# Earlier first gathers, a split last gather, full-partition compression and a reordered query norm in a two-layer transformer kernel

## The chip, the cores and the metric

The kernel runs on one core of one Trainium2 chip. The metric is the device time of one launch in microseconds (us). Three runs of the kernel before gave 3327.53, 3336.08 and 3337.21 us (median 3336.08).

## The reference

The input is a sequence of 256 tokens of width 2048, in float32. Two layers and a last norm are computed.

```python
# layer 1: four attention groups of 8 heads of 64 each, then an MLP
u = rmsnorm(h, norm_attn); p = split(u @ w_in)
o_mla = mla_mixer(...)      # c_q is normed (q_norm) before w_uq
o_fox = fox_mixer(...)      # forgetting attention, bias from a cumulative sum
o_nsa = nsa_mixer(...)      # compressed + selected + windowed attention
o_swa = swa_mixer(...)      # windowed, with sinks
h = h + rmsnorm(concat(o)) @ w_out
h = h + square(relu(rmsnorm(h) @ w_up)) @ w_down

def nsa_compress(kv, pos_emb, w1, w2):     # for keys and for values, 2 kv heads
    blk = kv[:, :, idx] + pos_emb          # 15 windows of 32 tokens, stride 16
    return gelu(blk.reshape(b, g, 15, 32 * 64) @ w1) @ w2

# layer 2: retention + RG-LRU, cross-attention to 256 memory rows, then experts
def peer_ffn(xn, w_q, sub_keys, u_tab, v_tab):
    q = xn @ w_q                            # 8 heads x 2 halves of 128
    vals, ids = top_k(q . sub_keys, 16)     # per token, head and half, of 128 keys
    top_sc, pos = top_k(vals0 + vals1, 16)  # of the 256 pairs
    eid = id0 * 128 + id1                   # 128 experts for each token
    act = gelu(x . u_tab[eid])              # 2048-long dot products
    return sum(softmax(top_sc) * act * v_tab[eid])
```

The last step is `rms_norm(h, final_norm)`.

## The kernel before

All engines run programs written out by hand and are tied by semaphores. Activations stand transposed, width on the 128 partitions and the 256 tokens on the free axis. Large products go in "chunks": a weight load of 1 MB lands in a ring of three slots (issued by SP), ACT rounds each half of it (128 x 1024) into `wh`, DVE takes the remainder into `wl` (L1690), and TensorE does three matmuls for each of 8 k-tiles of a half (L555 to L557; L617 to L619 with tokens as rows). Three halves of `wh`/`wl` rotate. `weave` interleaves the projections with the mixers on every engine by fixed ratios of `yield` steps, so what an engine does next is fixed by the code.

**The start of the mixers.** TensorE turns a column of factors (L517) and then wants the squares of the query latent `cq` for its norm (L498, `norm_sums`). In ACT's `mixers()` the copy of the factors, the copy of the bias row (`brow`), and the issue of its DMA come ahead of `squares("cq", cq)`.

**The compression.** `kc` and `vc` hold both kv heads, head g on partitions 64g to 64g+63. DVE builds `blk` (128 x 32 x 15, four additions at L1921), then TensorE does, for keys and again for values, 32 positions x 2 heads matmuls with 64 rows, 64 columns of weights and 15 moving columns (L782); a gelu on ACT and a second small product (L793, L798) follow. The relative-position biases (3 loads of 1 MB from DRAM into `bias`, issued by POOL at L2356) wait until the outputs of the first two mixers (`cqm`, which lives in `bias`) are moved away by DVE (L1908).

**The experts.** `first_queries` computes the queries of head 0 for token tile 0 (L955), their scores against the sub-keys (L1008), and turns the normed rows (L1000). DVE's `topk(0)` then gives 16 expert numbers a token (`eid`, L2248). There are 256 "rows" n (2 token tiles x 128 experts); for each, POOL issues an indirect DMA (L2368) that brings for 128 tokens one row of the table `uv` (2 MB: 2048 of u, 2048 of v). Row n lands in a buffer `BUF[n]`; five buffers rotate up to row `FEW` = 80, seven after it. A gather waits until the row that last used its buffer is added. DVE does the dot product (L2261, `dot`), ACT three small steps (`weigh`: gelu, times gate, a diagonal of weights), TensorE four matmuls of 512 columns (L1025, `sum_row`) that add into one of two PSUM tiles `sums`. Between rows TensorE does quarter chunks of the remaining queries (L981, `steps_before(n)` of them before row n, 16 before row 0), their weights coming through SP (`in_w_pq`, 1 MB each). The top-16 of later heads runs on DVE in four pieces before rows n with n % 16 in `TOP_AT` = (0, 2, 4, 6). `finish(t)` norms the sums of a tile: a square over 2048 columns with its sum on ACT, a mean on DVE, a root on ACT (after a table load), reciprocal and two products of 1024 columns on DVE (L2273), and two stores through SP (L2416).

## Time and profile before

| | us |
|---|---|
| median of three runs | 3336.08 |
| profiled execution | 3331.21 |
| its span | 3329.4 |
| PE / DVE / ACT / POOL busy | 3042.9 / 1924.9 / 1279.9 / 372.0 |

The profiled execution is 1.8 us longer than its span. By the page's row of DMA tenths the DMA engines are about half busy up to slice 24 of 40 (some 2000 us) and full from there to the last slice; TensorE is at nine tenths up to the same place and at seven tenths after it. A busy engine isn't the bound by itself: what counts in each stage is which wait ends last.

### The profile page before, as it was taken

To read this page: it belongs to the slowest core of one execution; us is meant where nothing else is said; L and a number is where in the kernel's file an instruction comes from. 1 tells how busy PE (TensorE), PEld (TensorE's weight loads), DVE (VectorE), ACT (ScalarE), POOL (GpSimd) and SP (SyncE) were. 2 spreads that over 40 slices of the span, in tenths; PEclk is the share of its full clock that TensorE was granted. 3 is DMA by queue.
4 is the path that set the end of the run, shared out by engine and by line. 5 is a ranking of instruction groups with operands and counts; after the bars stand their busy time and mean duration, and the time that the engine had idled before them with its cause. 6 is when DMAs were issued, how large, how long until landed. Compare 5 with 4: busy or idle time off the path is not lost.

```text
span 3329.4 us, 43391 instructions
## 1 busy us (share of the span) xinstructions
PE 3042.9 (91%) x18036; PEld 2379.4 (71%) x18036; DVE 1924.9 (58%) x2872; ACT 1279.9 (38%) x2355; POOL 372.0 (11%) x364
## 2 busy tenths in 40 slices
PE   8999999999999999999999999999987777777776
PEld 8888978999999999989999997444442233333332
DVE  6565665555555555676765454555555555555654
ACT  4554554444434345565544352222222222222222
POOL 1001000000000001100000011222232222222221
PEclk9999999999999999999999999999999989999999
DMA  7454446555555555544445448999999999999997
GB/s 216 174 195 158 161 151 215 179 188 179 188 179 186 181 182 198 195 165 153 152 177 203 140 152 333 430 431 430 431 430 431 430 429 431 431 431 431 431 431 337
DMA packets 94785, 912.65 MB, mean 274 GB/s; under 512 B 10416, under 2 KB 14904, under 8 KB 19580
## 3 DMA queue, kind: packets, MB, share of 16 engines
q0 software_dynamic: 38128, 541.61, 38.1%
q1 hardware_dynamic: 48816, 344.95, 29.9%
q10 hardware_dynamic: 7644, 23.30, 2.2%
q8 instruction: 142, 2.33, 0.3%
q14 instruction: 55, 0.45, 0.0%
HBM read 900.38 MB, written 9.45 MB: 273 GB/s over the span
## 4 chain that ended last, share of the span: by engine, by line
PE 66%; DMA 23%; DVE 6%; ACT 4%; issue 1%; ACTq 0%; POOL 0%; DVEq 0%; POOLq 0%
PE sums L555 15%; PE sums L557 14%; PE sums L556 14%; DMA area<-in_uv,cst 13%; PE sums L1025 9%; DMA hT<-in_uv,cst 5%; DMA ringx<-in_uv,cst 3%; PE sums L981 2%; DVE area L2261 1%; PE sums L617 1%; DVE wl L1690 1%; PE sums L619 1%; PE sums L618 1%; ACT cst L1070 1%; ACT area L1070 1%
## 5 line engine op out<-in xcount | busy, mean ns | idle before, releaser
L1690 DVE TENSOR_TENSOR wl<-ring,wh 128x1024 fp32r<-128x1024 f32 x612 | 749.9, 1230 | 597.2 <-ACT wh L1070 596.3
L1070 ACT ACTIVATE wh<-ring 128x1024 fp32r<-128x1024 f32 x612 | 643.5, 1054 | 460.2 <-PE sums L557 404.5
L1070 ACT ACTIVATE cst<-cst 128x1 f32<-128x1 f32 (+2 forms) x786 | 234.2, 299 | 903.6 <-DVE cst L2261 845.1
L1025 PE MATMUL sums<-area,cst 128*128 128x512 f32 x984 | 457.4, 611 | 100.1 <-ACT cst L1070 99.8
L1025 PEld LDWEIGHTS sums<-area,cst 128*128 128x128 f32 x984 | 182.7, 193 | 356.6 <-issue 189.6
L2261 DVE CUSTOM_DVE_ANT_0 area<-area 128x2048 f32<-128x2048 f32 x123 | 281.8, 2291 | 254.5 <-DMA area<-in_uv,cst 254.5
L555 PE MATMUL sums<-normed,wh 128*128 128x256 f32 x1440 | 407.0, 283 | 0.2 <-DVE wl L1690 0.2
L557 PE MATMUL sums<-normed,wl 128*128 128x256 f32 x1440 | 406.7, 282 | 0.0
L1025 PE MATMUL sums<-ringx,cst 128*128 128x512 f32 x656 | 303.8, 609 | 60.0 <-ACT cst L1070 60.0
L555 PE MATMUL sums<-hidden,wh 128*128 128x256 f32 x1024 | 289.8, 283 | 0.0
L556 PE MATMUL sums<-hidden,wh 128*128 128x256 f32 x1024 | 289.8, 283 | 0.0
L557 PE MATMUL sums<-hidden,wl 128*128 128x256 f32 x1024 | 289.8, 283 | 0.0
L556 PE MATMUL sums<-normed,wh 128*128 128x256 f32 x1024 | 289.8, 283 | 0.0
L2261 DVE CUSTOM_DVE_ANT_0 ringx<-ringx,area 128x2048 f32<-128x2048 f32 x82 | 187.9, 2291 | 170.7 <-DMA ringx<-in_uv,cst 170.7
L1025 PEld LDWEIGHTS sums<-ringx,cst 128*128 128x128 f32 x656 | 122.0, 192 | 229.4 <-issue 127.5
L555 PEld LDWEIGHTS sums<-normed,wh 128*128 128x128 f32 x1440 | 275.6, 191 | 0.5 <-issue 0.5
L557 PEld LDWEIGHTS sums<-normed,wl 128*128 128x128 f32 x1440 | 275.6, 191 | 0.0
L555 PE MATMUL sums<-inputs,wh 128*128 128x256 f32 x896 | 261.4, 292 | 2.2 <-DVE wl L1690 2.2
L557 PE MATMUL sums<-inputs,wl 128*128 128x256 f32 x896 | 253.3, 283 | 0.0
L2339 POOL TENSOR_TENSOR ssq<-ssq,sqb 128x256 f32<-128x256 f32 x75 | 56.4, 752 | 1661.2 <-ACT sqb L1070 1659.1
L556 PE MATMUL sums<-inputs,wh 128*128 128x256 f32 x848 | 239.8, 283 | 0.0
L2368 POOL DMA_INDIRECT area<-in_uv,cst x123 | 146.5, 1191 | 471.4 <-PE sums L1025 452.9
(335 smaller groups left out, 5753.6 us busy)
## 6 DMA issues: line engine op xcount, KB each, us to landing
ring<-in_w_in_a SPq DMA_DIRECT2D x66, 1024.0 KB, 4.9
ring<-in_w_up SPq DMA_DIRECT2D x64, 1024.0 KB, 4.9
ring<-in_w_down SPq DMA_DIRECT2D x64, 1024.0 KB, 4.9
ring<-in_w_out SPq DMA_DIRECT2D x32, 1024.0 KB, 5.0
ring<-in_w_in_b SPq DMA_DIRECT2D x16, 1024.0 KB, 4.9
ring<-in_w_xk SPq DMA_DIRECT2D x16, 1024.0 KB, 5.2
ring<-in_w_xv SPq DMA_DIRECT2D x16, 1024.0 KB, 5.1
ring<-in_w_xq SPq DMA_DIRECT2D x16, 1024.0 KB, 5.0
```

Source lines behind the costliest of these rows:

```text
L555: te.matmul(bank[:, 0:T], wh[:, j % 3, x], hi[:, k, :], start=k == 0, stop=False)
L556: te.matmul(bank[:, 0:T], wh[:, j % 3, x], lo[:, k, :], start=False, stop=False)
L557: mm = te.matmul(bank[:, 0:T], wl[:, j % 3, x], hi[:, k, :], start=False, stop=k == 15)
L617: te.matmul(b[t][:, :], hi[:, k, y], wh[:, j % 3, x], start=k == 0, stop=False)
L618: te.matmul(b[t][:, :], hi[:, k, y], wl[:, j % 3, x], start=False, stop=False)
L981: mm = te.matmul(bank[:, y], slots3[s][:, k * P:(k + 1) * P], xn[:, k, y], start=k == 0, stop=k == 15)
L1025: mm = te.matmul(sums[t][:, 512 * i:512 * i + 512], diag[:, n % 2, :], v[:, 512 * i:512 * i + 512], start=False, stop=n % 128 == 127)
L1070: return sc.activation(out, in_, f, **kw)
L1690: ve.tensor_tensor(wl[:, j % 3, :], ring[:, load % 3, j % 2 * 1024:j % 2 * 1024 + 1024], wh[:, j % 3, :], ALU.subtract).then_inc(lo_in, 1)
L2261: ve.tensor_tensor_reduce(u, u, xrow[:, t, :], 1.0, 0.0, ALU.mult, ALU.add, dots[:, t, s:s + 1]).then_inc(dotted, 1)
L2339: gp.tensor_tensor(acc[:, :], acc[:, :], sqb[:, j % 4, :], ALU.add).then_inc(acc_in, 1)
L2368: gp.indirect_dma_start(rowbuf[BUF[n]], None, A["uv"], bass.IndirectOffsetOnAxis(ap=eid[:, t, s:s + 1], axis=0)).then_inc(rows_in[BUF[n]], 16)
```

## The change

1. Experts, first rows: the scores of head 0, tile 0 are computed and evicted in two halves, the first in the middle of the second query chunk. `first_two()` gives the expert numbers of rows 0 and 1 right after the first eight of each half are known (the best pair, and the better of the two next candidates), so POOL gathers these two rows ahead of the rest of the top-16. DVE has nine more small instructions there.
2. Experts, order: 12 quarter chunks before row 0 instead of 16, then one for each row up to 5, then one for every two rows; five buffers up to row 110 instead of 80; the pieces of the top-16 stand before rows 8 to 11 of each 16 for the first seven, then at 0, 2, 4, 6 as before. ACT evicts scores after a row's weights instead of before them.
3. Experts, end: row 255 is gathered in two halves: u into its buffer, v (behind row 249) into the upper half of another. TensorE counts its four matmuls one by one; ACT squares 512 columns at a time with the root's table loaded ahead; DVE multiplies by the gain before the factor is known; the last factor is applied in two halves, 1024 columns by ACT and 1024 by DVE, stored by two queues.
4. Compression: weights and positions are laid out so that even and odd positions share the 128 partitions. TensorE first swaps the partition halves of `kc` and `vc` by four matmuls of 256 columns; DVE makes `blk` with eight additions of 64 x 8 x 15 for each of keys and values, before the copies of the mixer outputs; TensorE then does 16 matmuls of 128 rows, 64 weight columns and 30 moving columns for each instead of 64.
5. Biases: `cqm` moves out of `bias`; the three bias loads become six of half the size, the first three behind the forgetting rows, the last three once the second mixer has used its scores.
6. ACT's `squares("cq", cq)` comes before the copies and the DMA issue.
7. `cst` loses a table that was not used, so one early load falls from 1623 KB to 855 KB.

```diff
-        FEW = 80
-        BUF = ([0, 1, 2, 3, 4] * (FEW // 5) + [5, 0, 1, 2, 3, 4, 6] * 26)[:256]
+        FEW = 110
+        BUF = ([0, 1, 2, 3, 4] * (FEW // 5) + [5, 0, 1, 2, 3, 4, 6] * 21)[:256]
...
-        TOP_AT = (0, 2, 4, 6)
+        LATE = 249
+        def top_at(g):
+            return (8, 9, 10, 11) if g < 7 else (0, 2, 4, 6)
         def steps_before(n):
-            return min(64, 16 + 5 * n // 8)
+            return 12 + n if n < 5 else min(65, 17 + (n - 5) // 2)
...
+                off(on, EVICTED["nsa"] - 1)
+                on.wait_ge(out_off, 8)
+                for j, src in enumerate((kc, vc)):
+                    for g in range(2):
+                        mm = te.matmul(banks[6 + j][64 - 64 * g:128 - 64 * g, T:2 * T], ident[:, 64 * g:64 * g + 64],
+                                       src, start=True, stop=True)
+                    mm.then_inc(cmp_mm, 1)
...
-                    on.wait_ge(cmpw_in[j], 16 * len(cmp_w[j]))
-                    on.wait_ge(out_off, 8)
-                    on.wait_ge(blk_in, 2 * j + 2)
-                    for l in range(32):
-                        w, at = (cmp_w[1][1], l - 20) if j and l >= 20 else (cmp_w[j][0], l)
-                        for g in range(2):
-                            r = slice(64 * g, 64 * g + 64)
-                            mm = te.matmul(banks[6 + j][r, 0:15], w[r, at * 64:at * 64 + 64], blk[r, l, :],
-                                           start=l == 0, stop=l == 31)
+                    on.wait_ge(cmpw_in[j], 16)
+                    on.wait_ge(blk_in, 8 * j + 8)
+                    for i in range(16):
+                        mm = te.matmul(banks[6 + j][0:64, 0:30], cmp_w[j][:, i * 64:i * 64 + 64], blk[j][:, i, :],
+                                       start=i == 0, stop=i == 15)
                     mm.then_inc(cmp_mm, 1)
                     yield
-                    w2 = w2p[:, 64 * j:64 * j + 64]
+                    w2 = w2p[0:64, 64 * j:64 * j + 64]
...
+                        elif k == 8:
+                            on.wait_ge(keys_in, 16)
+                            on.wait_ge(qp_in, 1)
+                            on.wait_ge(rd_mean, RD_MEANS["ffn"])
+                            sub_scores(0, (0,), (0,))
...
-                on.wait_ge(keys_in, 16)
                 on.wait_ge(qp_in, 2)
-                on.wait_ge(rd_mean, RD_MEANS["ffn"])
-                sub_scores(0, (0,))
+                sub_scores(0, (0,), (1,))
                 off(on, len(EVICTIONS) - 1)
...
+                b, nth = (BUF[LATE], NTH[LATE] + 1) if n == 255 else (BUF[n], NTH[n])
+                v = rowbuf[b][:, DM:2 * DM]
                 on.wait_ge(weighed, n + 1)
+                on.wait_ge(rows_in[b], 16 * nth)
                 for i in range(4):
                     mm = te.matmul(sums[t][:, 512 * i:512 * i + 512], diag[:, n % 2, :], v[:, 512 * i:512 * i + 512],
                                    start=False, stop=n % 128 == 127)
-                mm.then_inc(added, 1)
+                    if n == 255 or i == 3:
+                        mm.then_inc(added, 1)
             biases()
...
+                on.wait_ge(off_v, EVICTED["cq"])
+                squares("cq", cq)
                 column(1)
                 on.wait_ge(brow_mm, 1)
                 act(brow[0:16, :], banks[3][0:16, :], ACT.Copy).then_inc(brow_in, 1)
...
+            def finish_last():
+                on.wait_ge(fin_v, 3)
+                act(pst[:, 3:4], ident[:, 0:1], ACT.Sqrt).then_inc(a_seq, seq.one())
+                for i in range(4):
+                    y = slice(512 * i, 512 * i + 512)
+                    on.wait_ge(added, 256 + i)
+                    act(xrow[:, 1, y], sums[1][:, y], ACT.Square, accum_out=sq4[:, i:i + 1]).then_inc(fin_a, 1)
+                on.wait_ge(fin_v, 7)
+                on.wait_ge(a_seq, seq.n)
+                act(pst[:, 3:4], pst[:, 2:3], ACT.Sqrt).then_inc(fin_a, 1)
+                on.wait_ge(fin_v, 9)
+                act(final[1][:, 0:1024], final[1][:, 0:1024], ACT.Copy, scale=pst[:, 3:4]).then_inc(fin_a, 1)
+                on.wait_ge(fin_a, 8)
+                sc.dma_start(A["out"][P:2 * P, 0:1024], final[1][:, 0:1024]).then_inc(out_in, 16)
...
+            def blocks(j, src):
+                on.wait_ge(small_in, 32)
+                off(on, EVICTED["nsa"] - 1)
+                on.wait_ge(cmp_mm, j + 1)
+                own, swapped = (x.rearrange("p (c l) -> p l c", l=16) for x in (src, banks[6 + j][:, T:2 * T]))
+                for s in range(2):
+                    r = slice(64 * s, 64 * s + 64)
+                    for g in range(2):
+                        x = own if g == s else swapped
+                        for a in range(2):
+                            at = slice(8 * a, 8 * a + 8)
+                            ve.tensor_tensor(blk[j][r, at, 15 * g:15 * g + 15], x[r, s::2, a:a + 15],
+                                             w2p[r, 128 + 16 * j + 8 * a:136 + 16 * j + 8 * a].unsqueeze(2)
+                                             .to_broadcast([64, 8, 15]), ALU.add).then_inc(blk_in, 1)
...
+            def first_two():
+                x = eq[:, 0, :]
+                own(ve.tensor_copy(idf[:, :, 0:2], ids[:, :, 0:2]))
+                on.wait_ge(v_seq, seq.n)
+                ve.scalar_tensor_tensor(eid[:, 0, 0:1], idf[:, 0, 0:1], 128.0, idf[:, 1, 0:1], ALU.mult,
+                                        ALU.add).then_inc(eid_in, 1)
+                for a in range(2):
+                    b = 1 - a
+                    own(ve.tensor_tensor(x[:, a:a + 1], vals[:, 0, a:a + 1], vals[:, 1, b:b + 1], ALU.add))
+                    own(ve.scalar_tensor_tensor(x[:, 2 + a:3 + a], idf[:, 0, a:a + 1], 128.0, idf[:, 1, b:b + 1],
+                                                ALU.mult, ALU.add))
+                on.wait_ge(v_seq, seq.n)
+                own(ve.tensor_tensor(x[:, 4:5], x[:, 0:1], x[:, 1:2], ALU.is_ge))
+                own(ve.tensor_tensor(x[:, 5:6], x[:, 2:3], x[:, 3:4], ALU.subtract))
+                on.wait_ge(v_seq, seq.n)
+                ve.scalar_tensor_tensor(eid[:, 0, 1:2], x[:, 5:6], x[:, 4:5], x[:, 3:4], ALU.mult,
+                                        ALU.add).then_inc(eid_in, 1)
...
-                on.wait_ge(scr_in, h + 2 if g else 1)
+                if g:
+                    on.wait_ge(scr_in, h + 3)
                 for c in range(2):
+                    if g == 0:
+                        on.wait_ge(scr_in, c + 1)
                     s = scr[:, h, 256 * t + P * c:256 * t + P * c + P]
                     own(ve.max(vals[:, c, 0:8], s))
                     on.wait_ge(v_seq, seq.n)
                     own(ve.max_index(ids[:, c, 0:8], vals[:, c, 0:8], s))
                     on.wait_ge(v_seq, seq.n)
+                    if g == 0 and c == 1:
...
+                if g == 15:
+                    x = eq[:, 0, 0:1]
+                    own(ve.scalar_tensor_tensor(x, sel[:, 0, 15:16], 128.0, sel[:, 1, 15:16], ALU.mult, ALU.add))
+                    on.wait_ge(v_seq, seq.n)
+                    for a in range(2):
+                        own(ve.tensor_scalar(eid2[:, a:a + 1], x, 2.0, float(a), ALU.mult, ALU.add))
+                    on.wait_ge(v_seq, seq.n)
+                e0 = 0 if g else 2
+                ve.scalar_tensor_tensor(eid[:, t, 16 * h + e0:16 * h + 16], sel[:, 0, e0:16], 128.0,
+                                        sel[:, 1, e0:16], ALU.mult, ALU.add).then_inc(eid_in, 1)
...
+            def finish_last():
+                on.wait_ge(grow_in, 16)
+                def times(i):
+                    y = slice(512 * i, 512 * i + 512)
+                    on.wait_ge(fin_a, 3 + i)
+                    ve.tensor_tensor(final[1][:, y], sums[1][:, y], grow[:, y], ALU.mult).then_inc(fin_v, 1)
+                for i in range(3):
+                    times(i)
+                on.wait_ge(fin_a, 6)
+                own(ve.tensor_reduce(pst[:, 2:3], sq4, AX.X, ALU.add))
+                on.wait_ge(v_seq, seq.n)
+                ve.tensor_scalar(pst[:, 2:3], pst[:, 2:3], 1.0 / DM, EPS, ALU.mult, ALU.add).then_inc(fin_v, 1)
+                times(3)
+                on.wait_ge(fin_a, 7)
+                ve.reciprocal(pst[:, 3:4], pst[:, 3:4]).then_inc(fin_v, 1)
+                on.wait_ge(fin_v, 9)
+                ve.tensor_scalar(final[1][:, 1024:2048], final[1][:, 1024:2048], pst[:, 3:4], None,
+                                 ALU.mult).then_inc(fin_v, 1)
...
+            def biases(h):
+                for x, d in ((0, 0), (1, 1), (2, 0)):
+                    view = bass.AP(bias_d.tensor, h * 128 * 513 + 255 - 128 * d, [[512, 128], [128 * 513, 8], [1, 128]])
+                    gp.dma_start(bias[:, h:h + 8, x * 128:x * 128 + 128], view).then_inc(bias_in, 16)
...
+            biases(0)
+            on.wait_ge(bias_in, 48)
+            on.wait_ge(biased, 16)
+            biases(8)
...
-                on.wait_ge(eid_in, n // 16 + 1)
-                gp.indirect_dma_start(rowbuf[BUF[n]], None, A["uv"],
-                                      bass.IndirectOffsetOnAxis(ap=eid[:, t, s:s + 1], axis=0)
-                                      ).then_inc(rows_in[BUF[n]], 16)
+                on.wait_ge(eid_in, n + 1 if n < 2 else n // 16 + 3)
+                if n < 255:
+                    gp.indirect_dma_start(rowbuf[BUF[n]], None, A["uv"], which(eid[:, t, s:s + 1])).then_inc(rows_in[BUF[n]], 16)
+                else:
+                    gp.indirect_dma_start(rowbuf[BUF[n]][:, 0:DM], None, halves, which(eid2[:, 0:1])
+                                          ).then_inc(rows_in[BUF[n]], 16)
+                    on.wait_ge(added, LATE + 1)
+                    gp.indirect_dma_start(rowbuf[BUF[LATE]][:, DM:2 * DM], None, halves, which(eid2[:, 1:2])
```

The order of DVE's instructions around the compression, before; `m1l` is the remainder of the memory rows, `wl` that of a weight half, `xn` takes the mixer outputs, `blk` the windows:

```order
L1744 SCALAR_TENSOR_TENSOR m1l<-area,x1l 128x256 x8
L1690 TENSOR_TENSOR wl<-ring,wh 128x1024
L1908 COPY xn<-area 128x256 x4
L1690 TENSOR_TENSOR wl<-ring,wh 128x1024
L1908 COPY xn<-area 128x256 x4
L1690 TENSOR_TENSOR wl<-ring,wh 128x1024
L1912 TENSOR_SCALAR nsink<-sinks 128x8
L1690 TENSOR_TENSOR wl<-ring,wh 128x1024
L1921 TENSOR_TENSOR blk<-area,w2p 128x240 x2
L1690 TENSOR_TENSOR wl<-ring,wh 128x1024
L1921 TENSOR_TENSOR blk<-area,w2p 128x240 x2
```

and after (`area` holds the windows there):

```order
L1779 SCALAR_TENSOR_TENSOR m1l<-area,x1l 128x256 x8
L1725 TENSOR_TENSOR wl<-ring,wh 128x1024
L1895 TENSOR_TENSOR area<-area,w2p 64x8x15 x2
L1895 TENSOR_TENSOR area<-sums,w2p 64x8x15 x4
L1895 TENSOR_TENSOR area<-area,w2p 64x8x15 x2
L1962 COPY xn<-cst 128x256 x4
L1725 TENSOR_TENSOR wl<-ring,wh 128x1024
L1895 TENSOR_TENSOR area<-area,w2p 64x8x15 x2
L1895 TENSOR_TENSOR area<-sums,w2p 64x8x15 x4
L1895 TENSOR_TENSOR area<-area,w2p 64x8x15 x2
L1962 COPY xn<-cqm 128x256 x4
L1725 TENSOR_TENSOR wl<-ring,wh 128x1024
L1965 TENSOR_SCALAR nsink<-sinks 128x8
L1725 TENSOR_TENSOR wl<-ring,wh 128x1024 x4
```

Sixteen shorter additions now stand ahead of the copies and of two `wl`, and none stands behind the last one shown.

TensorE's order where the experts begin, before: L955 is a query chunk of tile 0, L1008 scores, L1000 the turned rows, L981 query chunks, L1015 the residual that starts the sums, L1025 the weighted rows of v:

```order
L961 MATMUL sums<-cst,ssq 128x1 x2
L955 MATMUL sums<-xn,ring 128x128 x16
L1008 MATMUL sums<-area 128x128 x2
L1000 MATMUL sums<-cst,xn 128x128 x32
L981 MATMUL sums<-xn,ring 128x128 x32
L1008 MATMUL sums<-area 128x128 x2
L981 MATMUL sums<-xn,ring 128x256 x32
L1008 MATMUL sums<-area 128x128 x4
L1015 MATMUL sums<-cst,hT 128x128 x16
L1025 MATMUL sums<-area,cst 128x512 x8
L981 MATMUL sums<-xn,ring 128x256 x4
```

and after (the same steps are L968, L1023, L1015, L999, L1030 and L1042):

```order
L974 MATMUL sums<-cst,ssq 128x1 x2
L968 MATMUL sums<-xn,ring 128x128 x8
L1023 MATMUL sums<-area 128x128
L968 MATMUL sums<-xn,ring 128x128 x8
L1023 MATMUL sums<-area 128x128
L1015 MATMUL sums<-cst,xn 128x128 x32
L999 MATMUL sums<-xn,ring 128x128 x32
L1023 MATMUL sums<-area 128x128 x2
L999 MATMUL sums<-xn,ring 128x256 x16
L1030 MATMUL sums<-cst,hT 128x128 x16
L1042 MATMUL sums<-area,cst 128x512 x4
L999 MATMUL sums<-xn,ring 128x256 x4
```

The first scores moved into the middle of the second chunk, and one wide chunk and four score matmuls now stand behind the first rows instead of ahead of them.

ACT's last instructions, before:

```order
L1070 ACTIVATE cst<-cst 128x1 x2
L1070 ACTIVATE cst<-cst 128x128
L1070 ACTIVATE area,cst<-sums 128x2048
L1070 ACT_TABLE_LOAD
L1070 ACTIVATE cst<-cst 128x1
```

and after:

```order
L1088 ACTIVATE cst<-cst 128x1 x2
L1088 ACTIVATE cst<-cst 128x128
L1088 ACT_TABLE_LOAD
L1088 ACTIVATE cst<-cst 128x1
L1088 ACTIVATE area,cst<-sums 128x512 x4
L1088 ACTIVATE cst<-cst 128x1
L1088 ACTIVATE xn<-xn,cst 128x1024
L1581 DMA out<-xn 128x1024
```

The table load and a first root stand ahead of the squares, and a product and a store have come to ACT.

## Rows read from the trace of the kernel before

**Rows 1.** Windows: us, length, busy of each engine, PE clock, DMA share, GB/s

```profile
600.00:1000.00 400.00, 400.00 (x3334) 399.95 (x3333) 216.50 (x263) 177.85 (x221) 4.43 (x6) 1.00 0.54 182
2200.00:2400.00 200.00, 183.09 (x522) 97.65 (x523) 113.15 (x181) 46.56 (x138) 45.69 (x39) 0.98 1.01 431
2800.00:3270.00 470.00, 362.94 (x771) 142.39 (x770) 268.34 (x392) 101.08 (x308) 105.03 (x96) 0.98 1.01 431
```

**Rows 2.** Timeline of PE: start, us, instruction; idle before it, releaser

```profile
57.24 0.50 PE L517 MATMUL sums<-cst,rd 128*128 128x1 f32 x4
59.78 2.53 PE L498 MATMUL sums<-sqb,cst 128*128 128x256 f32 x6 [2.04 <-ACT sqb L1070]
```

**Rows 3.** Timeline of ACT there

```profile
57.98 0.59 ACT L1070 ACTIVATE area<-sums 16x512 f32<-16x512 f32 x1
58.60 0.67 ACTq L1247 DMA_DIRECT2D bias_rows<-area  x1
59.31 1.03 ACT L1070 ACTIVATE sqb<-area 128x256 f32<-128x256 f32 x3 [0.74 <-ACT area L1070]
```

**Rows 4.** Windows of 10 us where the PE clock falls

```profile
60.00:70.00 10.00, 9.87 (x58) 8.89 (x58) 6.66 (x8) 4.27 (x9) 0.00 (x0) 0.83 0.88 104
300.00:310.00 10.00, 8.00 (x136) 7.79 (x134) 2.12 (x3) 1.42 (x2) 2.10 (x2) 0.63 0.99 316
310.00:320.00 10.00, 9.37 (x162) 8.93 (x162) 2.17 (x3) 1.52 (x3) 0.00 (x0) 0.84 0.50 190
320.00:330.00 10.00, 10.00 (x78) 9.25 (x77) 3.53 (x5) 3.71 (x7) 0.00 (x0) 0.85 0.36 120
```

**Rows 5.** Timeline of PE from the norms to the late heads

```profile
236.34 1.99 PE L498 MATMUL sums<-sqb,cst 128*128 128x256 f32 x8 [0.54 <-ACT sqb L1070]
...
302.26 6.79 PE L782 MATMUL sums<-blk,area 64*64 64x15 f32 x128 [2.00 <-DVE blk L1921]
...
316.21 4.21 PE L782 MATMUL sums<-blk,area 64*64 64x15 f32 x128 [0.63 <-DVE blk L1921]
...
326.44 0.93 PE L669 MATMUL sums<-area 64*128 64x128 f32 x8
```

**Rows 6.** Timeline of DVE there

```profile
293.82 1.75 DVE L1690 TENSOR_TENSOR wl<-ring,wh 128x1024 fp32r<-128x1024 f32 x1
...
301.11 1.01 DVE L1921 TENSOR_TENSOR blk<-area,w2p 128x240 f32<-128x240 f32 x2
```

**Rows 7.** Window around the first gathers

```profile
2018.00:2030.00 12.00, 11.63 (x86) 10.95 (x85) 6.56 (x24) 4.03 (x9) 3.87 (x4) 1.00 0.62 221
```

**Rows 8.** Timelines of PE, DVE and POOL from the first scores to row 5

```profile
2013.41 0.68 PE L1008 MATMUL sums<-area 128*128 128x128 f32 x4 [0.41 <-issue]
...
2014.70 0.29 DVE L2206 MAX8 cst<-area 128x8 f32<-128x128 f32 x1 [3.70 <-ACT area L1070]
...
2024.47 0.17 DVE L2248 SCALAR_TENSOR_TENSOR cst<-cst 128x16 int32<-128x16 f32 x1
...
2044.07 2.27 DVE L2261 CUSTOM_DVE_ANT_0 area<-area 128x2048 f32<-128x2048 f32 x1
...
2024.92 1.04 POOL L2368 DMA_INDIRECT area<-in_uv,cst  x1 [17.34 <-DVE cst L2248]
...
2051.43 1.85 POOL L2368 DMA_INDIRECT area<-in_uv,cst  x1 [20.48 <-PE sums L1025]
```

**Rows 9.** Timelines of DVE, PE and ACT at the end

```profile
3312.93 2.29 DVE L2261 CUSTOM_DVE_ANT_0 ring<-ring,area 128x2048 f32<-128x2048 f32 x1 [2.56 <-DMA ring<-in_uv,cst]
...
3323.79 2.48 DVE L2273 SCALAR_TENSOR_TENSOR xn<-sums,cst,area 128x1024 f32<-128x1024 f32 x2
...
3316.34 3.70 PE L1025 MATMUL sums<-ring,cst 128*128 128x512 f32 x8 [1.16 <-ACT cst L1070]
...
3320.07 1.88 ACT L1070 ACTIVATE area<-sums 128x2048 f32<-128x2048 f32 x1 [3.79 <-PE sums L1025]
...
3322.06 1.28 ACT L1070 ACT_TABLE_LOAD   x1
```

179 lines of the change are left out of this document (82 added, 97 removed).

## Prediction

> **What bounds the kernel now.** I read the windows by stage first, then the waits of the engine that leads in each, then the chain of waits, to see whether such a wait stands on it. Up to about 2005 us TensorE leads: in a stretch of 400 us it is busy for 400.00, with 3334 matmuls, so 0.12 us for each matmul of 256 columns, while the DMA share is 0.54 [rows 1]. There a time counts if TensorE works less, idles less, or keeps its clock. The expert stage is led by the DMA engines: the share is 1.01 at 430 to 431 GB/s, with five buffers (window 2200 to 2400) and with seven (2800 to 3270) [rows 1]. A row of 2.097 MB takes 4.87 us at that rate. In that stage only three things count: when the stream fills, whether it breaks, and what follows its last byte. The change touches both kinds of stage.
>
> **A, query norm first.** TensorE sat idle for 2.04 us before L498, released by ACT's squares [rows 2]. ACT spent that time on the bias row (0.59) and the issue of its DMA (0.67), then squared at 59.31 [rows 3]. Squares first, TensorE can go on right behind L517, some 1.9 us earlier. After the idle the PE clock fell: the window 60 to 70 shows 0.83 [rows 4], that is 1.7 us lost to half clock (1.2 instead of 2.4 GHz). Full gain 3.6. But ACT must round the next weight half and square `ckv` a little later, and TensorE wants both sooner than before; I estimate about 1 us of new wait. I take 2.5, between 0.5 (the wait comes back for the next norm, the clock falls all the same) and 3.6. The bias row's DMA starts some 3 us later; its readers come tens of us after it.
>
> **B, compression.** The stretch from the end of the projections at 300.26 (302.26 less the 2.00 idle) to the late heads at 326.44 lasts 26.2 us [rows 5]. TensorE's order puts 72 projection matmuls in it: 8.6 us at 0.12. The compression takes 6.79 + 4.21 = 11.0, the idles before it 2.00 + 0.63 = 2.6 [rows 5], the small second products 0.7 (estimate). Together 22.9; the other 3.3 are projections at half clock: the windows from 300 to 330 show 0.63, 0.84 and 0.85 [rows 4], and the same 128 passes took 6.79 in the first and 4.21 in the second [rows 5].
> After: 32 passes for each of the two instead of 128. At 33 ns a pass (4.21/128) that is 1.05 us; if twice the rows and columns doubled it, 2.1. I take 1.3 each, 2.6 for both. The swap adds four matmuls of 256 columns, 2.0 us by the like of L498 (1.99) [rows 5], but it stands where TensorE waits for DVE's `m1l` pieces, which it catches up with; I leave 0.35.
> DVE is the new risk. It works without a break there, finishing a `wl` at 295.57 (293.82 + 1.75) [rows 6]. A pair of old additions (240 elements each) took 1.01 us [rows 6]. Eight new ones of 120 elements: at least half of 0.5 each, 2.0 us; at most the same 0.5 each, 4.0. I take 2.5 for keys and 2.5 for values. The first eight stand behind that `wl` and ahead of four copies (0.9) and the next `wl` (1.2), which then ends at 300.1; TensorE wants it at about 298.9, so it idles 1.3 us. The next `wl` ends at 304.7, when TensorE, through with the first compression, wants it at 304.8. Behind DVE's additions are queued only these `wl` halves, and TensorE alone waits for them; ACT isn't held up.
> New stretch: 8.6 + 2.6 + 0.7 + 0.35 + 1.3 = 13.6, a gain of 12.6. With 4.0 us for each eight it is some 5 less, and if the clock falls again for as long as in A, 2 less: 5.5 at the low end. At the high end, with no new idle, 14. I take 12.
>
> **C, first rows.** Now scores start at 2013.41, `topk(0)` at 2014.70, the ids are there at 2024.64 and POOL issues row 0 at 2024.92 [rows 8]. After: the first scores come after 8 of 16 k-tiles, so ACT has them at about 2011.7, DVE is through its first set when the second arrives at 2014.5; two steps (0.7) and the first id (0.4) give 2015.6, and POOL issues row 0 at 2016.0, row 1 at 2017.2. The rest of `topk(0)` ends at 2024.2 for nine more small instructions and the earlier start. What this is worth isn't the 9 us of row 0 but the bytes moved before the stream is full: between 2018 and 2030 the engines moved 221 of 431 GB/s [rows 7], leaving 12 x (1 - 221/431) = 5.8 us free. Two rows (9.7 us) and a query load (2.4) fill that window whole, and rows 2 to 4 follow from 2024.5. Gain 5.5, with 3 if the first gathers start slowly, 7 if they start before 2018.
> Does the stream break later? Rows 0 to 4 and three query loads are 31.6 us of transfers, to about 2049. Row 5 needs row 0 added. Before, `dot(0)` was held until 2044.07 by a piece of the next top-16 and row 5 was issued at 2051.43 [rows 8]. Now no piece stands there, 12 steps instead of 16 stand ahead on TensorE, and row 0 is added at about 2040. So the cover grows. From there a row costs TensorE 3.4 us plus half a step of 1.7, 4.3 under 4.87. The four pieces of a top-16 (10.3 us) and four dots (9.1) fill rows 8 to 11 on DVE, 19.4 of 19.5 us, while four rows of transfers (19.5 us) are in flight behind: a row is added about 7.3 us after it lands, so some 12 us of delay are covered. Cost of item 2: nothing. The new wait of `sum_row` on the buffer holds up only TensorE's own next matmuls and is met when the weight is.
>
> **D, the end.** The last row landed at 3312.93; dot, weight and a wait put its matmuls at 3316.34, 1.16 us after TensorE was free; they end at 3320.04 [rows 9]. With u landing half a row (2.4 us) before v, its weight is ready before TensorE has added row 254. So not 2.4 but only 1.2 are gained. Then 2048 columns of square (1.88 and 0.2 for the sum), a mean, a table load (1.28), a root, a reciprocal and 2.48 of products end at 3326.27 [rows 9]: 6.2 us. After: a square of 512 columns (0.6, estimate from 1.88), the sum 0.2, two small DVE steps 0.3, the last product with the gain 0.65 beside the root, reciprocal 0.15, 1024 columns on ACT 1.05, hops 0.3: 3.3 us. That is 2.9 less, of which I give back 0.9, as both halves of the output now start together instead of 1.2 us apart. D is 1.2 + 2.0 = 3.2, between 1 and 5.
> On the load of the table the row shows 1.28 us and the root at once behind it [rows 9]. The Trainium skill, "ScalarE: Activation LUTs", section "What ACT_TABLE_LOAD costs", adds a drain of about 1.38 us to each switch; by it the early load would save 2.7 and D would be 4.6. The trace shows no such drain, and I stay with 1.28.
> On the split gather the windows show the stream at its full rate with up to five gathers queued [rows 1]. The Trainium skill, "DMA: Bandwidth & Descriptors", section "Anatomy of one DMA — SWDGE (gpsimd) path", gives each transfer some 2.0 us of fixed time beside its bytes. If that were paid in line, the second half would land 2.0 later and D would be 1.2; against it speak the last dots, 4.85 us apart (2.29 and 2.56 idle) with 4.87 us of bytes in each [rows 9].
>
> **E, the rest.** Bias loads in six parts: the same 3 MB, the first 1.5 MB at about 95 to 105 us beside weight loads. The stage's DMA share is about half [rows 1], and a weight slot is refilled more than two halves ahead of its use, so nothing; up to 3 us if a weight load is late. The shorter load of `cst` helps no one who waits.
>
> **Sum.** 2.5 + 12 + 5.5 + 3.2 = 23.2. Against the profiled execution: 3331.2 - 23.2 = 3308.0. That execution stands 4.9 us under the median of the three, and the highest of them 6 over it; I predict **3309**, one us up for that. A difference of 0.3% (10 us) is about what a measurement of this kernel can tell from none; the median less that is 3326.
>
> **Rivals.**
> *TensorE's stages give little* (chance 0.17). DVE's additions take 4 us for each eight, TensorE idles on `wl`, and the idle brings the half clock back, as a wait of 2 us did twice here [rows 2, 4, 5]. Then A is 0.5 and B 5.5: 3331.2 - 0.5 - 5.5 - 5.5 - 3.2 = 3316.5. For it speaks DVE without a gap at 293.8; against it that the new idle is 1.3, and wide matmuls follow it.
> *The experts give nothing* (0.12). Early gathers push the query weights back, TensorE waits for them, buffers come free late, and the end follows from TensorE: C and D are 0, 3331.2 - 14.5 = 3316.7. For it: TensorE is busy 183 of 200 us in the window to 2400 [rows 1]. Against: the cover of 12 us.
> *Both* (0.04): 3331.2 - 6 = 3325.
> *Slower* (0.03). The top-16 pieces before rows 8 to 11 leave DVE 0.1 us of slack. If DVE falls behind by more than the 12 us of cover there, the first row of the next head is gathered late and the DMA engines idle, in each of seven heads. From 3.3 us a head on the whole gain is eaten; at 6 us: 3308 + 42 = 3350.
> *The forecast*: 0.64.
>
> **Numbers.** The forecast's own range is 3300 to 3317; the rivals at 3316 to 3325 stretch the upper side. Runs of one kernel lie 10 us apart, so I give 3297 to 3322. Faster by over 0.3% is nearly all of the forecast and of its first two rivals, less what the spread of the runs takes: 0.88. Within 0.3%: 0.09. Slower: 0.03.
>
> **What would show it.** A: no idle over 1 us before the first norm's matmuls, clock at 1.0 between 60 and 70. B: passes of the compression 1 to 2 us for each, late heads at about 311 to 314. C: the first gather issued some 9 us before the full `topk`, DMA share 1.0 from 2 us behind it, and the time from first gather's data to last landing unchanged per byte. D: 9 us or less from the landing of v to the last byte out. Wrong: any window of the expert stage with a share under 0.98; TensorE waiting for `wl` over 2 us near 300; a low clock near 305.

## The result and the profile after

| | before | after |
|---|---|---|
| median | 3331.81 us (4 runs, 3326.97 to 3337.21) | 3307.97 us (4 runs, 3307.00 to 3311.36) |
| profiled execution, its span | 3331.21, 3329.4 | 3307.08, 3304.7 |

The ratio is 0.9929, 95% interval 0.9917 to 0.9940: faster by 0.7%. The forecast was 3309.

The two traces are compared at landmarks that both have: the column of factors in front of the first norm (L517 / L523), the first chunk behind the norms (L725 / L731), the late heads (the first matmuls of the heads that follow the compression, L669 / L675), the first expert queries (L955 / L968), the landing of row 254 (the start of its dot, which waits for the DMA), the end of the span. The landmarks of before that stand in no group, in timelines of PE and DVE:

```profile
67.86 1.46 PE L725 MATMUL sums<-area 128*96 128x256 f32 x6
...
2005.24 3.73 PE L955 MATMUL sums<-xn,ring 128*128 128x128 f32 x32
...
3308.07 2.29 DVE L2261 CUSTOM_DVE_ANT_0 hT<-hT,area 128x2048 f32<-128x2048 f32 x1 [2.58 <-DMA hT<-in_uv,cst]
```

and in the timeline of PE after, from the first norm to the first queries:

```profile
56.54 0.50 PE L523 MATMUL sums<-cst,rd 128*128 128x1 f32 x4
56.91 1.54 PE L504 MATMUL sums<-sqb,cst 128*128 128x256 f32 x6
...
62.30 0.67 PE L504 MATMUL sums<-sqb,cst 128*128 128x256 f32 x2 [0.97 <-ACT sqb L1088]
...
64.23 1.46 PE L731 MATMUL sums<-area 128*96 128x256 f32 x6
...
287.53 1.08 PE L781 MATMUL sums<-area,cst 128*64 128x256 f32 x8
...
295.64 0.39 PE L561 MATMUL sums<-x1l,wh 128*128 128x256 f32 x1 [0.85 <-DVE wl L1725]
...
297.26 2.05 PE L791 MATMUL sums<-area 128*64 128x30 f32 x32
...
300.86 0.29 PE L802 MATMUL sums<-hk,w2p 64*64 64x15 f32 x4
...
304.13 2.05 PE L791 MATMUL sums<-area 128*64 128x30 f32 x32
...
311.12 0.93 PE L675 MATMUL sums<-area 64*128 64x128 f32 x8
...
1990.53 3.73 PE L968 MATMUL sums<-xn,ring 128*128 128x128 f32 x32
```

The idle of 2.04 us before the norm [rows 2] is gone and one of 0.97 has come at the next norm. Of the compression's 128 passes 32 are left, 2.05 us in all, and only 0.85 us of idle stands ahead. The PE clock no longer falls in any window that stood at 0.63 to 0.85 [rows 4] (us, length, busy of each engine, PE clock, DMA share, GB/s):

```profile
60.00:70.00 10.00, 9.03 (x65) 8.13 (x63) 7.01 (x10) 6.87 (x12) 0.00 (x0) 1.00 0.76 89
300.00:310.00 10.00, 10.00 (x100) 9.43 (x100) 3.39 (x3) 3.04 (x6) 0.00 (x0) 1.00 0.44 131
310.00:320.00 10.00, 10.00 (x87) 9.36 (x88) 6.38 (x13) 6.16 (x12) 0.00 (x0) 1.00 0.57 202
320.00:330.00 10.00, 10.00 (x87) 9.21 (x84) 6.64 (x16) 5.88 (x14) 0.00 (x0) 1.00 0.42 143
...
2018.00:2030.00 12.00, 12.00 (x57) 8.13 (x56) 2.74 (x4) 4.61 (x12) 1.93 (x1) 1.00 1.00 425
2200.00:2400.00 200.00, 179.57 (x492) 92.58 (x491) 111.73 (x181) 44.74 (x136) 40.80 (x39) 0.97 1.01 430
2800.00:3270.00 470.00, 359.65 (x771) 140.39 (x769) 267.91 (x391) 101.07 (x308) 99.22 (x96) 0.99 1.01 431
```

The last three rows stand at the times of [rows 7] and [rows 1]. The stream stays at its rate. The window from 2018 to 2030 isn't the same piece of work as before, since the first queries start 14.7 us earlier now; at the distance from them that [rows 7] has, from 2003.3 to 2015.3, the engines move 402 GB/s where they moved 221, that is 12 x (402 - 221)/431 = 5.0 us of stream. The stream starts earlier, as DVE and POOL show (the first two gathers wait for L2249 and L2260, the others for L2324):

```profile
1997.21 0.29 DVE L2272 MAX8 cst<-area 128x8 f32<-128x128 f32 x1 [0.93 <-ACT area L1088]
...
2008.93 0.17 DVE L2324 SCALAR_TENSOR_TENSOR cst<-cst 128x14 int32<-128x14 f32 x1
...
2001.16 1.03 POOL L2478 DMA_INDIRECT area<-in_uv,cst  x1 [8.30 <-DVE cst L2249]
2002.51 0.97 POOL L2478 DMA_INDIRECT area<-in_uv,cst  x1 [0.30 <-issue]
2009.38 0.94 POOL L2478 DMA_INDIRECT area<-in_uv,cst  x1 [5.90 <-DVE cst L2324]
...
2025.44 1.93 POOL L2478 DMA_INDIRECT area<-in_uv,cst  x1 [11.68 <-PE sums L1042]
```

At the end, to set beside [rows 9] (DVE, PE, ACT):

```profile
3287.25 2.29 DVE L2337 CUSTOM_DVE_ANT_0 ringx<-ringx,area 128x2048 f32<-128x2048 f32 x1 [2.57 <-DMA ringx<-in_uv,cst]
...
3289.71 2.29 DVE L2337 CUSTOM_DVE_ANT_0 ringx<-ringx,area 128x2048 f32<-128x2048 f32 x1 [0.17 <-DMA ringx<-in_uv,cst]
...
3299.60 0.76 DVE L2370 TENSOR_SCALAR xn<-xn,cst 128x1024 f32<-128x1024 f32 x1
...
3290.66 3.70 PE L1042 MATMUL sums<-ringx,cst 128*128 128x512 f32 x8 [1.17 <-ACT cst L1088]
3294.19 3.60 PE L1042 MATMUL sums<-hT,cst 128*128 128x512 f32 x8
...
3293.09 1.28 ACT L1088 ACT_TABLE_LOAD   x1
3294.38 0.20 ACT L1088 ACTIVATE cst<-cst 128x1 f32<-128x1 f32 x1
...
3299.60 1.15 ACT L1088 ACTIVATE xn<-xn,cst 128x1024 f32<-128x1024 f32 x1 [0.47 <-DVE cst L2368]
```

Row 255's matmuls now stand directly behind row 254's, and 6.9 us after the last of them (3297.79) the span ends; before it was 9.4 (3320.04 to 3329.4).

| stretch | before | after | gain | forecast |
|---|---|---|---|---|
| start to L517 / L523 | 57.24 | 56.54 | 0.7 | - |
| to the first chunk behind the norms | 10.62 | 7.69 | 2.9 | A 2.5 |
| to the late heads | 258.58 | 246.89 | 11.7 | B 12 |
| to the first queries | 1678.80 | 1679.41 | -0.6 | 0 |
| to the landing of row 254 | 1302.83 | 1296.72 | 6.1 | C 5.5 |
| to the end of the span | 21.33 | 17.45 | 3.9 | D 3.2 |
| sum | 3329.4 | 3304.7 | 24.7 | 23.2 |

The first and the fourth stretch hold no effect of the change: in the twelve kernels below the first landmark lies between 56.04 and 57.36, and the stretch from the late heads to the first queries takes 1677.2 to 1681.6 us, where their code is the same. Over such a stretch single profiles of the same code differ by up to 4 us, so each effect is read between near landmarks. From the first queries to the landing of row 254 the changed kernel and eight kernels below (the six with the same code there, late_blocks, adds2, cols15, late_bias, ends and whole_last, and old_pace and pieces10) take 1296.7 to 1297.9 us.

### The profile page after: what moved, and what is told of

Read it like the earlier page. It is cut to its first block, busy times and chain, and to the rows that moved or that the text cites. A ratio compares the mean times of both kernels' runs of the same rounds, so it can differ in the third digit from the quotient of the medians.

```text
span 3304.7 us, 43323 instructions
## 1 busy us (share of the span) xinstructions
PE 3030.5 (92%) x17852; PEld 2369.6 (72%) x17852; DVE 1929.5 (58%) x2900; ACT 1282.4 (39%) x2364; POOL 360.7 (11%) x368
## 4 chain that ended last, share of the span: by engine, by line
PE 66%; DMA 22%; DVE 7%; ACT 4%; issue 1%; ACTq 0%; POOL 0%; DVEq 0%; POOLq 0%
PE sums L561 15%; PE sums L563 15%; PE sums L562 15%; DMA area<-in_uv,cst 12%; PE sums L1042 9%; DMA ringx<-in_uv,cst 8%; DMA ring<-in_uv,cst 2%; PE sums L999 2%; DVE area L2337 2%; PE sums L623 1%; DVE wl L1725 1%; PE sums L625 1%; PE sums L624 1%; ACT cst L1088 1%; DVE ringx L2337 1%
## 5 line engine op out<-in xcount | busy, mean ns | idle before, releaser
L1042 PE MATMUL sums<-area,cst 128*128 128x512 f32 x1032 | 477.2, 609 | 96.4 <-ACT cst L1088 96.3
L2337 DVE CUSTOM_DVE_ANT_0 area<-area 128x2048 f32<-128x2048 f32 x129 | 295.6, 2292 | 269.4 <-DMA area<-in_uv,cst 269.4
L1042 PEld LDWEIGHTS sums<-area,cst 128*128 128x128 f32 x1032 | 192.4, 193 | 360.7 <-issue 198.5
L1042 PE MATMUL sums<-ringx,cst 128*128 128x512 f32 x680 | 323.8, 622 | 90.0 <-ACT cst L1088 90.0
L1042 PEld LDWEIGHTS sums<-ringx,cst 128*128 128x128 f32 x680 | 128.8, 196 | 272.7 <-ACT cst L1088 138.3
L2337 DVE CUSTOM_DVE_ANT_0 ringx<-ringx,area 128x2048 f32<-128x2048 f32 x86 | 197.1, 2291 | 184.5 <-DMA ringx<-in_uv,cst 184.5
L561 PEld LDWEIGHTS sums<-normed,wh 128*128 128x128 f32 x1440 | 275.6, 191 | 1.6 <-issue 1.5
L562 PEld LDWEIGHTS sums<-normed,wh 128*128 128x128 f32 x1024 | 196.6, 192 | 0.0
```

Source lines behind the costliest of these rows:

```text
L561: te.matmul(bank[:, 0:T], wh[:, j % 3, x], hi[:, k, :], start=k == 0, stop=False)
L562: te.matmul(bank[:, 0:T], wh[:, j % 3, x], lo[:, k, :], start=False, stop=False)
L1042: mm = te.matmul(sums[t][:, 512 * i:512 * i + 512], diag[:, n % 2, :], v[:, 512 * i:512 * i + 512], start=False, stop=n % 128 == 127)
L2337: ve.tensor_tensor_reduce(u, u, xrow[:, t, :], 1.0, 0.0, ALU.mult, ALU.add, dots[:, t, s:s + 1]).then_inc(dotted, 1)
```

## Experiments

All are edits of the changed kernel (3307.97). "Heads" is the start of the late heads less that of L523, 254.6 us in the changed kernel and 254.5 to 254.6 in the six runs below that leave this stretch as it is.

| kernel | median us | ratio to before, 95% | heads |
|---|---|---|---|
| no_early | 3312.06 | 0.9943, 0.9927 to 0.9960 | 254.5 |
| old_pace | 3306.99 | 0.9933, 0.9917 to 0.9950 | 254.5 |
| pieces12 | 3358.83 | 1.0080, 1.0063 to 1.0097 | 254.6 |
| pieces11 | 3319.76 | 0.9967, 0.9957 to 0.9977 | 254.6 |
| pieces10 | 3306.23 | 0.9925, 0.9908 to 0.9942 | 254.6 |
| late_blocks | 3310.92 | 0.9942, 0.9926 to 0.9959 | 259.3 |
| adds2 | 3315.80 | 0.9950, 0.9933 to 0.9967 | 261.2 |
| cols15 | 3313.57 | 0.9950, 0.9932 to 0.9967 | 261.2 |
| late_bias | 3307.80 | 0.9934, 0.9916 to 0.9952 | 255.4 |
| ends | 3314.73 | 0.9951, 0.9934 to 0.9968 | 257.3 |
| whole_last | 3309.82 | 0.9936, 0.9921 to 0.9951 | 254.6 |
| best | 3304.60 | 0.9918, 0.9905 to 0.9932 | 252.8 |

### Early rows: no_early

```diff
-                    if g == 0 and c == 1:
-                        first_two()
...
+                if g == 0:
+                    first_two()
                 e0 = 0 if g else 2
```

> The changed kernel with one move: first_two() runs at the end of topk(0) and not in its middle, so rows 0 and 1 are gathered with the others. The changed kernel's profiled execution took 3307.1 us; its first gather was issued at 2001.16, the full expert numbers came at 2008.93. Theory (bytes moved before the stream is full): the first gather is issued at about 2009.5, the DMA engines idle some 6 us more between 2002 and 2012 (query loads fill part of it), the stream ends as much later: 3312 to 3315. Rival (the gain of the expert stage came from the fewer TensorE steps ahead of row 0 and the later top-16 pieces, not from the two early rows): within 1 us, 3306 to 3308.

The first gather comes 17.98 us after the first queries (2010.27 less 1992.29), against 10.63. The window from 2002 to 2018 moves

```profile
2002.00:2018.00 16.00, 15.54 (x116) 14.67 (x115) 8.58 (x38) 6.57 (x13) 4.80 (x5) 1.00 0.56 215
```

with the changed kernel at 391 GB/s there. The first queries of this run start 1.8 us later than the changed kernel's; shifted by that, from 2003.8 to 2019.8, it moves 258 GB/s, and 16 x (391 - 258)/431 is 4.9 us of stream. From the first queries to the landing of row 254 it is 1301.63 us, 4.9 more. So 4.9 of the 6.1 us of C are the two early rows. The other 1.2 can be the scores in halves and the fewer steps ahead of row 0, but they are no more than this stretch scatters, so they aren't shown. The theory holds.

### The pace in the expert stage: old_pace, pieces12, pieces10, pieces11

```diff
-            return (8, 9, 10, 11) if g < 7 else (0, 2, 4, 6)
+            return (0, 2, 4, 6) if g else (8, 9, 10, 11)        # old_pace, and:
-            return 12 + n if n < 5 else min(65, 17 + (n - 5) // 2)
+            return 12 + n if n < 5 else min(65, 16 + 5 * n // 8)
...
+            return (12, 13, 14, 15) if g < 7 else (0, 2, 4, 6)  # pieces12; (10, ..., 13) and (11, ..., 14) alike
```

> The changed kernel with the top-16 pieces of heads 2 to 7 of the first tile before rows 0, 2, 4 and 6 of each 16 again (head 1's stay before rows 8 to 11), and from row 5 on 16 + 5n/8 TensorE steps again. Theory (item 2 costs and brings nothing, rows are hidden behind four in flight): 3306 to 3308, DMA share 1.0 throughout. Rival (the later pieces are part of the gain, as the old ones held up dots that freed buffers): the share falls in windows between 2100 and 2500 and the time is 3311 to 3316.

> The changed kernel with the pieces before rows 12 to 15 of each 16, in seven heads. In the changed kernel the ids of a head came at 2157.8, the gather that needs them was issued at 2169.35 when its buffer was free, and the rows in flight last to about 2176. Four rows later is 19.4 us, ids at 2177. Theory (a gather may be late until the rows in flight have landed): each of seven heads loses 3 to 5 us, 3328 to 3342, with the share below 1.0 once in each head. Rival 1 (no cover: every us past the moment at which the buffer is free counts): 7 x 7.8 = 55 us, 3362. Rival 2 (more cover than that, as DVE runs ahead without the pieces): nothing, 3307.

> The changed kernel with the pieces before rows 10 to 13 of each 16, in seven heads. With pieces before 12 to 15 a head's ids came at 2189.2, 3.5 us after its last row in flight had landed (2185.7) and 13.8 after the buffer was free (2175.4), and the kernel lost 51 us, 7.3 a head. Theory (a head loses the time from the last landing to the ids, plus about 4 us until the next bytes flow): two rows earlier is 9.7 us, ids 6.2 before the last landing, which is more than the 4: no loss, 3307 to 3309. Rival (every us past the moment at which the buffer is free counts, at 7.3/13.8 for one): ids 4.1 after that moment, 2.2 a head, 15 us: 3322.

> The changed kernel with the pieces before rows 11 to 14 of each 16, in seven heads, one row earlier than the run that lost 7.3 us a head. Theory (as for rows 10 to 13): ids 1.4 us before the last landing, 4 us until the next bytes flow, 2.5 us a head, 17 us: 3324. Rival (every us past the moment at which the buffer is free counts, at 7.3/13.8 for one): ids 8.9 after it, 4.7 a head, 33 us: 3340.

Old_pace is as fast, its share from 2100 to 2800 is 1.01: the pace neither costs nor brings. Pieces12 lost 50.9 us, 7.3 a head where I had expected 3 to 5, and near rival 1's number. Its rows don't show rival 1's mechanism, though (DVE and POOL; the dots are those of rows 30, 31 and 32):

```profile
2183.51 2.29 DVE L2337 CUSTOM_DVE_ANT_0 area<-area 128x2048 f32<-128x2048 f32 x1 [0.89 <-DMA area<-in_uv,cst]
...
2189.06 0.17 DVE L2324 SCALAR_TENSOR_TENSOR cst<-cst 128x16 int32<-128x16 f32 x1
...
2189.48 2.28 DVE L2337 CUSTOM_DVE_ANT_0 area<-area 128x2048 f32<-128x2048 f32 x1
...
2199.95 2.29 DVE L2337 CUSTOM_DVE_ANT_0 area<-area 128x2048 f32<-128x2048 f32 x1 [8.17 <-DMA area<-in_uv,cst]
...
2190.01 2.58 POOL L2478 DMA_INDIRECT area<-in_uv,cst  x1 [20.24 <-DVE cst L2324]
```

The buffer had been free since 2175.4, 13.8 us before the ids (2189.2), so rival 1 would take 13.8 us here. Row 30 landed at 2183.51 and row 31, the last in flight, a row of transfers later, at about 2188.4, 0.9 us before the ids. (The expectations for pieces10 and pieces11 have it at 2185.7, four times 4.85 behind row 27 at 2166.3; they leave out a load of 1 MB of query weights that landed at 2182.2.) Row 32 landed at 2199.95: 11.6 us after row 31 instead of 4.85, 6.7 lost in this head. In windows of 1 us the DMA engines moved nothing from 2188 to 2193. Row 32's bytes flowed from 2195.1 on (a row less than its landing, and the windows are full from 2195), 5.9 us after the ids; I had allowed 2 to 4. Part of that is POOL: its issue took 2.58 us instead of the usual 0.94 and ended 0.8 us behind the dot that DVE was doing.

The last two kernels bracket it. In pieces11 the dots are those of rows 30 to 32:

```profile
2174.01 0.17 DVE L2324 SCALAR_TENSOR_TENSOR cst<-cst 128x16 int32<-128x16 f32 x1
...
2174.55 2.29 DVE L2337 CUSTOM_DVE_ANT_0 area<-area 128x2048 f32<-128x2048 f32 x1
...
2179.39 2.29 DVE L2337 CUSTOM_DVE_ANT_0 area<-area 128x2048 f32<-128x2048 f32 x1 [2.54 <-DMA area<-in_uv,cst]
...
2186.87 2.29 DVE L2337 CUSTOM_DVE_ANT_0 area<-area 128x2048 f32<-128x2048 f32 x1 [5.18 <-DMA area<-in_uv,cst]
```

The ids are there 5.2 us before row 31 lands (1.4 in my expectation), and row 32 lands 7.5 us after it, 2.6 lost here; in all 11.8 us, 1.7 a head. In pieces10 the ids (2166.6) are 11.1 us before row 31 lands (2177.73; I had 6.2), row 32 follows 4.84 us later, and nothing is lost.

The rival falls, and pieces11 is what decides: the buffer was free at 2166.4, 7.8 us before the ids, which at 7.3/13.8 is 4.1 us a head, 29 in all, for a measured 11.8. In pieces10 the ids came only 1.8 us after the buffer was free, not 4.1, so by its own rule the rival would lose 7 us there and not 15; nothing was lost.

My theory keeps its form and not its number. Counted back from row 32's landing, its bytes flow 5.9 us after the ids in pieces12 and 7.8 in pieces11; by windows of 1 us the engines are back at full rate some 5.8 us after the ids in both (from 2195 and from 2180). So ids may come until about 6 us (at most 8) before the last row in flight lands, not 4.

In the changed kernel the ids come 20.8 us before row 31 lands (2157.8, 2178.6), so they could come 13 to 15 us later. That is not the forecast's cover of 12 us, which counts from the moment at which the buffer is free: from there the ids may be late by 5 to 7 us (7.8 and 13.8 late, 2.6 and 6.7 lost). And in the changed kernel it is the buffer that is late: row 32's gather is issued at 2169.35, 9.2 us before row 31 lands, and from the issue to the flow it took 5 to 7 us in the two late kernels. What is left there is 2 to 4 us.

### The compression: late_blocks, adds2, cols15

```diff
# late_blocks: the additions behind "?nsa", where they stood before
-                    blocks(j, (kc, vc)[j])
...
+                    if j < 2:
+                        blocks(j, (kc, vc)[j])
# adds2: every addition twice, the second time behind the first; TensorE waits for both
-                    on.wait_ge(blk_in, 8 * j + 8)
+                    on.wait_ge(blk_in, 16 * j + 16)
...
-                for s in range(2):
+                for p, s in ((0, 0), (0, 1), (1, 0), (1, 1)):
...
+                    on.wait_ge(blk_in, 16 * j + 8 * p)
# cols15: each pass of 30 columns as two of 15
-                    for i in range(16):
-                        mm = te.matmul(banks[6 + j][0:64, 0:30], cmp_w[j][:, i * 64:i * 64 + 64], blk[j][:, i, :],
-                                       start=i == 0, stop=i == 15)
+                    for g, i in [(g, i) for g in range(2) for i in range(16)]:
+                        mm = te.matmul(banks[6 + j][0:64, 15 * g:15 * g + 15], cmp_w[j][:, i * 64:i * 64 + 64],
+                                       blk[j][:, i, 15 * g:15 * g + 15], start=i == 0, stop=i == 15)
```

> The changed kernel with DVE's sixteen additions for the compression behind the copies and the wl halves, where the old ones stood, and the swap on TensorE where it is now. The compression's passes are 32 for each of the two as in the change. Theory (the gain of that stretch is partly the place: waits for the additions and the half clock that follows them): TensorE waits 2 us or more for them again, the PE clock falls below 0.9 in a window between 295 and 320, and the late heads start 3 to 6 us later than the 311.12 of the changed kernel: 3310 to 3313. Rival (the gain is in the fewer passes alone): late heads within 1 us of 311.12, 3307 to 3308.

> The changed kernel with each of the sixteen additions done twice (eight, then the same eight again, for keys and for values), 2.1 us more DVE work ahead of each of two wl halves. Theory (DVE's slack there is used up, TensorE already waits 0.85 us for a wl at 295.6): the wait for the first wl grows by 2.1, that for the next comes to 1 to 2, and an idle over 2 us brings half clock: late heads at 315 to 318 against 311.12, time 3311 to 3314. Rival (the additions are hidden, TensorE's wait has another cause): late heads within 1 us, 3307 to 3308.

> The changed kernel with each compression pass of 30 columns split in two passes of 15 columns with the same 128 x 64 weights, so 32 matmuls of 15 columns in place of 16 of 30 for each of keys and values; in the profile a pass is half an instruction pair. The changed kernel took 2.05 us for each. Theory 1 (the columns set the time of a pass): each compression stays at 2.0 to 2.3 us and the time at 3307 to 3308. Theory 2 (loading weights sets it, whatever the columns): each compression takes 4.1 us, the late heads start 4 us later, 3311.

PE in late_blocks, and its window from 300 to 310 (columns as above, clock 0.69):

```profile
299.75 3.59 PE L791 MATMUL sums<-area 128*64 128x30 f32 x32 [3.00 <-DVE area L1895]
```

```profile
300.00:310.00 10.00, 10.00 (x82) 9.55 (x82) 2.95 (x8) 1.70 (x4) 0.00 (x0) 0.69 0.22 88
```

The same two views of adds2:

```profile
298.43 0.38 PE L561 MATMUL sums<-x1l,wh 128*128 128x256 f32 x1 [3.06 <-DVE wl L1725]
...
300.57 3.62 PE L791 MATMUL sums<-area 128*64 128x30 f32 x32
```

```profile
300.00:310.00 10.00, 10.00 (x66) 9.45 (x65) 6.76 (x18) 1.70 (x4) 0.00 (x0) 0.52 0.54 193
```

PE in cols15:

```profile
298.11 3.90 PE L791 MATMUL sums<-area 128*64 128x15 f32 x64
...
306.84 4.24 PE L791 MATMUL sums<-area 128*64 128x15 f32 x64
```

and its windows of PE alone (us, length, busy, clock, DMA share, GB/s) where the clock falls:

```profile
308.00:310.00 2.00, 2.00 (x38) 1.00 0.00 0
310.00:312.00 2.00, 2.00 (x17) 0.56 0.00 0
312.00:314.00 2.00, 2.00 (x12) 0.50 0.00 0
```

Late_blocks: with the additions where they had been, TensorE waits 3.00 us for them, the clock is 0.50 from about 300 to 306, and the heads are 4.7 us later. So of B's 11.7 us about 4.7 are the place of the additions; the other 7, by difference, are the fewer passes and what else changed there. The time rose by 3.0 only, within what the later stretches scatter.

Adds2: 2.1 us more of DVE work lengthened TensorE's wait from 0.85 to 3.06 us, and the clock was at 0.5 to about 309: the heads came 6.6 us later, 2.2 from the wait and the other 4.4 with the clock. No second wait for `wl` came, which I had expected too: TensorE at half clock wanted it later. The rival of my prediction (TensorE's stages give little) was thus 2 us of DVE work away. The mechanism is right; the time rose by 7.8 us, and I had said 3 to 6.

Cols15: a pass of 15 columns takes 61 and 66 ns (the last 0.9 us of the second run are at half clock), one of 30 columns 64 (2.05/32). Columns do not set the time. So theory 2 holds as far as that goes: with 128 rows x 64 columns of weights a pass costs this much. The passes of before, 64 x 64, took 33 (4.21/128, the last 0.8 us of them at half clock too). Whether the rows loaded set it, or the two halves of the partitions worked side by side before, no run tells. The heads come 6.6 us later, of which 4.0 are the passes. The rest is a low clock that begins near the end of the second run of narrow passes with no idle ahead of it (PE is busy for all of 308 to 314). The first run, of 3.90 us and 1.6 us behind an idle of 0.85, left the clock at 1.00, so such a run doesn't always do it, and what decides isn't shown. Before, the clock also fell a second time, near the end of narrow passes behind an idle of 0.63 [rows 4, 5].

### Bias loads and the two ends: late_bias, ends, whole_last

```diff
# late_bias: behind POOL's subtractions for the memory rows
-            biases(0)
-            on.wait_ge(bias_in, 48)
             on.wait_ge(biased, 16)
-            biases(8)
...
+            biases(0)
+            biases(8)
# ends: squares("cq", cq) behind brow's DMA again, and finish(1) in place of finish_last()
# whole_last: row 255 in one gather
-                b, nth = (BUF[LATE], NTH[LATE] + 1) if n == 255 else (BUF[n], NTH[n])
+                b, nth = BUF[n], NTH[n]
```

> The changed kernel with both sets of bias loads (3 MB) issued late, behind POOL's subtractions for the memory rows, about 290 us, as before. Theory (the early loads bring nothing by themselves): late heads at 311 to 312, 3307 to 3308. Rival (3 MB at about 300 us take the DMA share to 1.0 there, as in the kernel before, and hold back weight loads or the late heads' biases): TensorE waits for wl or the heads for the bias, 1 to 4 us: 3308 to 3311.

> The changed kernel with two far apart parts undone: at the start ACT copies the bias row and issues its DMA before the squares of the query latent; at the end the old finish (one square of 2048 columns, table load behind it, products on DVE, two stores through SP) with the last row still gathered in two halves. Theory: the first undoing costs 3.6 us, read at the first weight chunk behind the norm (64.23 in the changed kernel) and still there at the late heads (311.12) and the first queries; the second costs 2.5 us between the last matmul and the end (6.9 us in the changed kernel, 9.4 in the one before): 3313. Rival (the stages between have waits that take an early start back): the late heads start within 1 us of 311.12 and the time is 3309.5.

> The changed kernel with the last row gathered whole, as one transfer into its own buffer; the new finish stays. In the changed kernel u of the last row landed at 3289.71, its matmuls began at 3294.19 directly behind those of row 254. Theory: the whole row lands at about 3292.1, dot 2.29 and weight 0.95 later its matmuls begin at 3295.4, 1.2 us later: 3308.3. Rival (a transfer costs some 2 us besides its bytes, so two halves are dearer than one): the whole row lands within 0.5 us of the dot of the half, and the end comes at the same time or up to 1 us earlier, 3306 to 3307.

Late_bias: the same time (3307.80), but the heads are 0.8 us later, more than the 0.1 that they scatter. TensorE waits 1.57 us for `wl` instead of 0.85, since DVE's copies ahead of it took 1.59 us, not 0.90, while POOL issued the loads (busy for 5.00 us of the window 290 to 295). So the early bias loads are worth 0.8 us of B's 11.7, by a way that neither the forecast nor my rival had. In the time it doesn't show, as E forecast.

Ends: L731 comes 10.47 us after L523 (7.69 in the changed kernel, 10.62 before), the idle is 2.04 again and the window 60 to 70 shows the clock at 0.92. The first part thus costs 2.8, not 3.6: I had read 3.6 off absolute times, with the 0.7 by which starts differ in it. The heads are 2.7 later, so nothing of it is given back by there, and the rival falls. From the last matmul (3301.39) to the end it is 9.4 us: the second part costs 2.5. Together they cost 5.3 us by the landmarks and 6.8 by the medians; the other 1.5 are no more than the long stretches and the runs scatter.

Whole_last: row 254 landed at 3289.33, the last matmul ended at 3301.29, 11.96 us later against 10.54. The split of the last row is worth 1.4 us. The whole row landed at 3294.18, 4.85 us behind row 254, and the half 2.46 behind it, each for its bytes, so the rival falls.

### A further version: best

```diff
+                squares("ckv", ckv, False)      # ahead of the next wh; its root stays behind
...
+                blocks(0, kc); yield; take(0, "mla"); blocks(1, vc); yield; take(1, "fox")
...
+                b, nth = (BUF[n - 5], NTH[n - 5] + 1) if n >= 254 else (BUF[n], NTH[n])
...
-                act(final[1][:, 0:1024], final[1][:, 0:1024], ACT.Copy, scale=pst[:, 3:4]).then_inc(fin_a, 1)
+                act(final[1][:, 0:768], final[1][:, 0:768], ACT.Copy, scale=pst[:, 3:4]).then_inc(fin_a, 1)
```

> The changed kernel with four more edits: ACT squares the key latent ahead of the next weight half (TensorE idled 0.97 us for it at 62.3); DVE's copies of the first mixer stand behind the next wl half (0.85 us idle at 295.6); the last two rows are both gathered as u and v, v into the buffers of rows 249 and 250, so the dots of both come half a row earlier; of the last products ACT takes 768 columns and DVE 1280. Theory: 1.0 + 0.85 + 0.9 + 0.2 = 2.9 us, 3304. Rival (each idle comes back at the next want of TensorE, and at the end TensorE's two rows of 3.6 us stay as late as the landing allows): 3306 to 3307.

Both idles are gone and the heads are 1.8 us earlier, as expected. From the landing of row 253 to the end it is 21.5 us (3282.99 to 3304.5) against 22.3 (3282.38 to 3304.7), 0.8 for 1.1 expected. The median is 3.4 us lower, but the intervals of the two ratios overlap: the landmarks show the gains, the times alone do not.

## Why the prediction was right

*What bounds it.* Both stage rules held: where TensorE leads each idle, each pass and each stretch at half clock counted in full (A was still there at the late heads, B in the sum), and in the expert stage only the start, the breaks and the end counted.

*A, 2.5 taken, 2.9 measured.* The mechanism is as written, with a new wait of about 1 us (0.97). The clock did not fall after it, so the loss to half clock was saved whole.

*B, 12 taken, 11.7 measured.* I had the stretch at 13.6 us with the idle and the swap in it. From the first pass to the late heads it is 13.9, and the idle of 0.85 and the swap of 1.08 ahead of it put the first pass only 0.6 us later against the first landmark behind the norms than the end of the projections was before (233.0 and 232.4). Two sizes were off, in opposite directions: a compression takes 2.05 us and not 1.3 (the lower end from 33 ns a pass lay nearer to my choice than the doubling, which was right), and the idle is 0.85 and not 1.3, as eight additions take 2.1 us and not 2.5. The 3.3 us of half clock did come back; the forecast laid them at the door of the idle alone, and cols15 shows that narrow passes can bring the fall without one. Of the 11.7 us 0.8 are the early bias loads (late_bias), which the forecast had at nothing.

*C, 5.5 taken, 6.1 measured.* The reading "free bytes in the window, not the 9 us of row 0" was right: the two early rows gave 4.9. The first gather came 10.6 us after the first queries, 10.8 in my steps. That item 2 cost nothing is right, but the cover of 12 us behind it was mis-sized. It was 19.5 us of transfers less 7.3 from landing to added, and took a gather's bytes to flow as soon as it was issued; the two late kernels took 5 to 7 us from issue to flow, and from the moment at which the buffer is free only 5 to 7 us were covered. What was left in the changed kernel is 2 to 4 us, so the term came out right with less room than the forecast said, and in that a part is luck.

*D, 3.2 taken, 3.9 measured.* The split gives 1.4 (1.2) and the finish 2.5 (2.0). From the last matmul to the end of the last product it was 6.2 us (3320.04 to 3326.27) and is 3.0 (3297.79 to 3300.75, on ACT), 3.3 less where I had 2.9. From there to the end of the span it was 3.1 and is 3.9: of the 0.9 that I gave back for the two stores 0.8 came. The row of the table load agrees with the 1.28 us that I stayed with: the root stands at 3294.38, directly behind a load that began at 3293.09. The split gather cost no 2 us in line either, since u landed 2.46 us after row 254, for half of 4.87 us of bytes.

*The rivals.* None came in. "TensorE's stages give little" needed 2.1 us more of DVE work (adds2). "The experts give nothing" wanted TensorE to hold the buffers back; the share stayed at 1.01, and no run makes that case. "Slower" needed ids too late for the next head: two rows later cost nothing, three cost 12 us, four 51, and the kernel was then slower than before (1.008), by the mechanism that I had named.

*The base.* The gains were taken from one profiled execution, 3331.21, and one us was added; the median of before had been 3336.08 in three runs and is 3331.81 in four. The forecast's 23.2 us is the part that was worked out; the medians moved by 23.8. The four terms together came to 24.6 by the landmarks, 1.4 more than forecast. That 3309 lies only 1.0 from the measured 3307.97 owes something to a base that held.

## What to carry to other kernels

Split a stage by who leads it and read each effect between two near landmarks, not from the start of the trace: starts differ by 1.3 us and a long stretch by 4 with the same code. In a stream that never empties a late request costs nothing until the last transfer in flight is here some 6 us from landing, and from then on every microsecond, at every repetition; count the time from the request to its bytes into the cover. An idle or a run of narrow matmuls on TensorE can be paid twice, once itself and once in the half clock that sometimes follows, so a small delay on the engine that feeds it can cost three times its length (adds2: 2.2 us more of idle, 6.6 us in all).

## What the runs showed of the hardware

- TensorE's granted clock fell to 0.5 (1.2 of 2.4 GHz) after idles of 2.00, 2.04, 3.00 and 3.06 us, and not after 0.85, 0.97 and 1.57. Around 2 us it isn't settled by the length: an idle of 2.10 us at the same place, about 527 us, was followed by the low clock in best (0.57 from 527 to 531) and not in pieces10 (1.00), and 2.20 us at 542.95 in the kernel before left it at 1.00. It also fell near the end of 64 passes of 15 columns in 4.24 us with no idle (cols15). It stayed low for some 7 us (late_blocks, cols15) to 10 us (adds2).
- A float32 pass over 128 x 64 weights took 64 ns at 30 columns and 61 to 66 at 15; one over 64 x 64 weights 33 at 15 (with 0.8 of 4.21 us at half clock).
- From the ids of a gather to its bytes at full rate it took 5.8 us where the ids came too late (pieces11, pieces12), against 2.4 us for the first gather of the kernel before (ids 2024.64, full windows from 2027). With gathers queued it did not show (rows land 4.85 us apart).
- Of the 48 gathers that POOL began to issue while DVE was in a dot, 47 ended about 0.81 us after that dot and took up to 3.0 us, in the kernel before, in the changed kernel and in old_pace alike; most others took 0.94.
- Four DVE copies of 128 x 256 took 1.59 us in place of 0.90, or 0.40 each in place of 0.22, while POOL issued six loads of 0.5 MB; the additions of 64 x 120 beside them kept their time (0.61 for two).
